# Projection weights laid out in memory one unit at a time, 4 KB in a row per partition

## What is computed

```python
mod = c @ w_ada + b_ada
shift, scale, gate = jnp.split(mod, 3, axis=-1)
h = rmsnorm(x, pre_norm_gain) * (1.0 + scale[:, None, :]) + shift[:, None, :]
proj = h @ w_in                                   # w_in: 1024 x 10840
(aq, ak, av, az, iq, ik, iw, bq, bk, bv, bz, bbeta, ba, ga, gb) = jnp.split(proj, points, axis=-1)
...
y_a = (o_a * jax.nn.silu(az)) @ w_a_out           # sparse attention, top 128 keys by an indexer
y_b = o_b.reshape(b, s, B_V_WIDTH) @ w_b_out      # gated delta rule in chunks
y = jax.nn.sigmoid(ga) * y_a + jax.nn.sigmoid(gb) * y_b
out = y @ w_o
return x + gate[:, None, :] * rmsnorm(out, post_norm_gain)
```

## Time and profile before

| | us |
|---|---|
| median of 3 runs | 827.98 (827.45 to 828.1) |
| profiled execution, span from first to last instruction | 824.1 |
| PE busy | 797.4 |
| PE weight load (beside the matmuls) busy | 639.8 |
| DVE, ACT, POOL busy | 439.9, 330.6, 393.3 |
| DMA queue's share of 16 engines' span | 40.2% |

### The profile page before, as it was taken

How to read it: one execution, slowest core, us unless ns; L and a number is a source line. 1 busy time by engine, 2 the same in 40 slices (tenths; PEclk the granted TensorE clock), 3 DMA queues, 4 the chain that set the end, 5 groups by cost and what they waited for, 6 DMA issues and landing times.

```text
span 824.1 us, 11189 instructions
## 1 busy us (share of the span) xinstructions
PE 797.4 (97%) x4060; PEld 639.8 (78%) x4060; DVE 439.9 (53%) x957; ACT 330.6 (40%) x701; POOL 393.3 (48%) x338
## 2 busy tenths in 40 slices
PE   6899899999999999999999999999999999999997
PEld 2377775787887888888887777777778788878997
DVE  5677779848779855776754333343343332331113
ACT  0557455543544435445335334424443322122231
POOL 0415643465545644545554453554365355434451
PEclk9999999999999999999999999999999999999999
DMA  8936656543344333333212212222222255542602
GB/s 314 345 104 213 163 116 168 157 118 104 95 82 113 72 103 104 89 89 90 78 51 78 78 52 76 83 74 75 77 77 73 61 173 182 176 128 77 215 17 102
DMA packets 166800, 95.61 MB, mean 116 GB/s; under 512 B 35009, under 2 KB 158274, under 8 KB 165722
## 3 DMA queue, kind: packets, MB, share of 16 engines
q1 hardware_dynamic: 166746, 94.91, 40.2%
HBM read 85.11 MB, written 9.22 MB: 114 GB/s over the span
## 4 chain that ended last, share of the span: by engine, by line
PE 77%; DVE 11%; DMA 4%; ACT 4%; issue 2%; SPq 1%; POOL 1%; DVEq 0%; POOLq 0%; ACTq 0%
PE ps L699 19%; PE ps L701 18%; PE ps L700 18%; DMA w_ada_sb<-in_w_ada 2%; PE ps L979 2%; PE ps L1030 2%; PE ps L1029 2%; PE ps L1028 2%; PE ps L966 2%; ACT prob L1278 2%; DVE prob L1917 1%; PE ps L973 1%; PE ps L817 1%; DVE kraw L1734 1%; PE ps L863 1%
## 5 line engine op out<-in xcount | busy, mean ns | idle before, releaser
L1376 POOL TENSOR_TENSOR w_lo<-raw,w_hi 128x512 fp32r<-128x512 f32 (+1 forms) x216 | 294.7, 1388 | 305.0 <-ACT w_hi L1052 289.6
L699 PE MATMUL ps<-h_hi,w_hi 128*128 128x512 f32 (+1 forms) x680 | 286.2, 421 | 1.1 <-DVE h_lo L1597 1.0
L701 PE MATMUL ps<-h_hi,w_lo 128*128 128x512 f32 (+1 forms) x680 | 266.7, 392 | 0.0
L700 PE MATMUL ps<-h_lo,w_hi 128*128 128x512 f32 (+1 forms) x680 | 265.4, 390 | 0.0
L699 PEld LDWEIGHTS ps<-h_hi,w_hi 128*128 128x128 f32 (+1 forms) x680 | 127.8, 188 | 32.1 <-issue 8.3
L701 PEld LDWEIGHTS ps<-h_hi,w_lo 128*128 128x128 f32 (+1 forms) x680 | 127.3, 187 | 28.8
L700 PEld LDWEIGHTS ps<-h_lo,w_hi 128*128 128x128 f32 (+1 forms) x680 | 128.1, 188 | 23.0 <-issue 2.2
L1052 ACT ACTIVATE w_hi<-raw 128x1024 fp32r<-128x1024 f32 (+1 forms) x109 | 113.6, 1051 | 19.4 <-PE ps L1030 17.1
L1218 ACT ACTIVATE o_tok<-ps 128x128 f32<-128x128 f32 x32 | 8.9, 278 | 92.8 <-PE ps L931 92.7
L1029 PE MATMUL ps<-w_lo,y_hi 128*128 128x256 f32 x128 | 36.2, 283 | 0.0
L1030 PE MATMUL ps<-w_hi,y_lo 128*128 128x256 f32 x128 | 36.2, 283 | 0.0
(11 more groups left out here) (276 smaller groups left out, 1330.7 us busy)
## 6 DMA issues: line engine op xcount, KB each, us to landing
raw<-in_w_in SPq DMA_DIRECT2D x84, 512.0 KB, 3.7
w_ada_sb<-in_w_ada SPq DMA_DIRECT2D x8, 1024.0 KB, 11.4
inverse_tiles<-zero SPq DMA_DIRECT2D x12, 344.0 KB, 4.8
raw<-in_w_b_out SPq DMA_DIRECT2D x8, 512.0 KB, 3.8
raw<-in_w_a_out SPq DMA_DIRECT2D x8, 512.0 KB, 3.8
ada<-in_w_ada SPq DMA_DIRECT2D x8, 512.0 KB, 5.0
raw<-in_w_o SPq DMA_DIRECT2D x8, 512.0 KB, 3.8
x_sb<-in_x SPq DMA_DIRECT2D x4, 512.0 KB, 20.0
```

The lines of the kernel that those rows point to most:

```text
L699: pe.matmul(out_ap, w_hi[:, slot, k, 0:m], rhs_hi(k), start=(k == 0), stop=False)
L700: pe.matmul(out_ap, w_hi[:, slot, k, 0:m], rhs_lo(k), start=False, stop=False)
L701: mm = pe.matmul(out_ap, w_lo[:, slot, k, 0:m], rhs_hi(k), start=False, stop=(k == KT - 1))
L1376: ins = pool.tensor_tensor(w_lo[:, slot, ks, 0:n], raw[:, slot, ks, 0:n], w_hi[:, slot, ks, 0:n].bitcast(F32), ALU.subtract)
```

## The change

The host hands over one new array, `w_units`, in place of the four matrices: unit by unit, each as `[128 partitions, 8, 128]`, so that a partition's 4 KB lie in a row and a unit is one block of 512 KB. Unit S is padded with zeros from 88 to 128 columns and read by the same `load`, in one DMA instead of two, so that its semaphore counts as the others' do. ACT, POOL and PE still use 88 columns of it. Nothing else is moved.

```diff
@@ -497,29 +497,11 @@
         sp.dma_start(small_cols[:, 48:56], a_log.rearrange("(a n) -> a n", a=1).to_broadcast([P, 8])).then_inc(s_sc, 16)
         sp.dma_start(small_cols[:, 56:64], dt_bias.rearrange("(a n) -> a n", a=1).to_broadcast([P, 8])).then_inc(s_sc, 16)
 
-        def columns(w, col):
-
-            return w.rearrange("(k p) n -> p k n", p=P)[:, :, col:col + P]
-
-        wv = w_in.rearrange("(k p) n -> p k n", p=P)
-        n_ik = IDX_DIM + IDX_HEADS
-        sp.dma_start(raw[:, 0, :, 0:n_ik], wv[:, :, COL_IK:COL_IK + n_ik]).then_inc(s_raw[0], 16)
-        sp.dma_start(raw[:, 0, :, n_ik:N_SMALL], wv[:, :, COL_BETA:COL_BETA + 2 * HEADS]).then_inc(s_raw[0], 16)
-        FIRST = {"K": COL_BK, "Q": COL_BQ, "V": COL_BV, "Z": COL_BZ, "I": COL_IQ, "GA": COL_GA, "GB": COL_GB, "AQ": COL_AQ,
-                 "AK": COL_AK, "AV": COL_AV, "AZ": COL_AZ}
-
         def load(q):
 
-            kind, n = UNITS[q]
-            if kind in FIRST:
-                src = columns(w_in, FIRST[kind] + n * P)
-            elif kind == "O":
-                src = columns(w_o, OUT_COLS[n])
-            else:
-                src = columns(w_b_out if kind == "BO" else w_a_out, n * P)
             if q >= RING:
                 sp.wait_ge(lo_made, q - RING + 1)
-            sp.dma_start(raw[:, q % RING, :, :], src).then_inc(s_raw[q % RING], 16)
+            sp.dma_start(raw[:, q % RING, :, :], w_units[q]).then_inc(s_raw[q % RING], 16)
 
         def clear(ns):
             sp.wait_ge(*pro_pool.at("zero"))
@@ -627,6 +609,7 @@
             sp.dma_start(ada[0][:], b_ada[2 * D:3 * D].rearrange("(a n) -> a n", a=1).to_broadcast([P, D])).then_inc(s_bc, 16)
             sp.dma_start(ada[1][:], post_gain.rearrange("(a n) -> a n", a=1).to_broadcast([P, D])).then_inc(s_bc, 16)
 
+        load(0)
         load(1)
         sp.dma_start(cst[:, 1:, :], cst_in[:, 1:, :]).then_inc(s_cst, 16)
         for q in range(2, RING):
@@ -1040,7 +1023,7 @@
         def split(q, n=P):
 
             slot = q % RING
-            act.wait_ge(s_raw[slot], (q // RING + 1) * 16 + (16 if slot == 0 else 0))
+            act.wait_ge(s_raw[slot], (q // RING + 1) * 16)
             if q == 0:
                 act.wait_ge(*pro_act.at("cos"))
                 act.wait_ge(*pro_act.at("sinI"))
@@ -2025,8 +2008,26 @@
                     *norm_dve.inc(f"x{n}{t}"))
 
 
-NAMES = ["x", "c", "positions", "w_ada", "b_ada", "pre_norm_gain", "post_norm_gain", "w_in", "idx_k_ln_gain",
-         "idx_k_ln_bias", "dn_conv_w", "dn_a_log", "dn_dt_bias", "dn_norm_gain", "w_a_out", "w_b_out", "w_o"]
+NAMES = ["x", "c", "positions", "w_ada", "b_ada", "pre_norm_gain", "post_norm_gain", "idx_k_ln_gain",
+         "idx_k_ln_bias", "dn_conv_w", "dn_a_log", "dn_dt_bias", "dn_norm_gain"]
+FIRST_COL = {"K": COL_BK, "Q": COL_BQ, "V": COL_BV, "Z": COL_BZ, "I": COL_IQ, "GA": COL_GA, "GB": COL_GB, "AQ": COL_AQ,
+             "AK": COL_AK, "AV": COL_AV, "AZ": COL_AZ}
+
+
+def unit_weights(q, w_in, w_a_out, w_b_out, w_o):
+
+    kind, n = UNITS[q]
+    if kind == "S":
+        w = np.zeros((D, P), np.float32)
+        w[:, 0:SM_BETA] = w_in[:, COL_IK:COL_IK + SM_BETA]
+        w[:, SM_BETA:N_SMALL] = w_in[:, COL_BETA:COL_BETA + 2 * HEADS]
+    elif kind in FIRST_COL:
+        w = w_in[:, FIRST_COL[kind] + n * P:FIRST_COL[kind] + (n + 1) * P]
+    elif kind == "O":
+        w = w_o[:, OUT_COLS[n]:OUT_COLS[n] + P]
+    else:
+        w = (w_b_out if kind == "BO" else w_a_out)[:, n * P:(n + 1) * P]
+    return w.reshape(KT, P, P).transpose(1, 0, 2)
 
 
 def kernel(**inputs):
@@ -2045,6 +2046,8 @@
         a = np.asarray(inputs[name])
 
         add(name, a if name in ("c", "positions") else a[0])
+    weights = [np.asarray(inputs[name])[0] for name in ("w_in", "w_a_out", "w_b_out", "w_o")]
+    add("w_units", np.stack([unit_weights(q, *weights) for q in range(len(UNITS))]))
     for name, a in zip(("masks", "rotary"), constants()):
         add(name, a)
     args.append(nc.dram_tensor("out", (S, D), F32, kind="ExternalOutput").ap())```

The new array is made before the launch, on the host. How SP's list changes, at the start of the program. Before (the numbers behind L are lines of the kernel before, `raw` is the ring of loaded weights, `cst` constants, `gc_rows` the decay rows in memory, `L` their copies on chip):

```order
L498 DMA small_cols<-in_dn_dt_bias 128x8
L506 DMA raw<-in_w_in 128x8x72
L507 DMA raw<-in_w_in 128x8x16
L522 DMA raw<-in_w_in 128x8x128
L631 DMA cst<-in_masks 128x896
L522 DMA raw<-in_w_in 128x8x128 x6
L528 DMA inverse_tiles<-zero 128x688 x3
L522 DMA raw<-in_w_in 128x8x128 x2
L639 DMA gc_rows<-gcT 8x512
L531 DMA L<-gc_rows 128x512 x4
```

More of the change, by code:

```diff
@@ L144, in inc, with build, program @@
         return self.sem, 1
-def build(nc, x, c, positions, w_ada, b_ada, pre_gain, post_gain, w_in, ln_gain, ln_bias, conv_w, a_log, dt_bias,
-          norm_gain, w_a_out, w_b_out, w_o, cst_in, cols_in, out):
+def build(nc, x, c, positions, w_ada, b_ada, pre_gain, post_gain, ln_gain, ln_bias, conv_w, a_log, dt_bias,
+          norm_gain, w_units, cst_in, cols_in, out):
     with ExitStack() as ctx:
[L150 to L155, removed]
+        program(nc, ctx, x, c, positions, w_ada, b_ada, pre_gain, post_gain, ln_gain, ln_bias, conv_w, a_log,
+                dt_bias, norm_gain, w_units, cst_in, cols_in, out)
+def program(nc, ctx, x, c, positions, w_ada, b_ada, pre_gain, post_gain, ln_gain, ln_bias, conv_w, a_log,
+            dt_bias, norm_gain, w_units, cst_in, cols_in, out):
     cursor = [-(-nc.sbuf_base // 64) * 64]
```

## The result

The changed kernel takes 829.82 us in the median of 20 runs (827.37 to 833.29), the kernel before, run beside it, 827.58 (826.87 to 832.28). The ratio is 1.0029, its 95% interval 1.0017 to 1.0040: 2.2 us slower, where I had forecast 827.2 us (825.8 to 829.0) and no visible change. (The ratios in this text are those on record for the runs; the quotient of the two medians differs from them by up to 0.1%.) The profiled execution spans 830.5 us (824.1 before); like those of before it is one execution of many, and a rather long one, so its 6.4 us are read as places where time is lost, and their worth in the median comes from the runs.

What follows compares the result with a forecast made beforehand. TensorE bounds the kernel, busy 797.4 of 824.1 us; prologue -0.6 and decay rows -0.2 give 823.3 in the profile, so the runs' median 827.98 - 0.8 = 827.2 us, range 825.8 to 829.0, no visible change.

Steps and rivals of the forecast that it cites:

- Step 3: Decay rows: the gc_rows store behind a unit load lands 0.4 us sooner, DVE can use 0.24: -0.2 us.
- Steps 1 and 4: SyncE's load issues, and all unit loads after the prologue, hidden beneath PE work: 0 us each.
- the signs of being wrong: ACT waiting for later units, first h_hi after 39.9, w_ada's landing moved, PE idle from 100 to 300 us changed over 1 us.
- step 2: Prologue: S and K0 land earlier, POOL's w_lo end sooner, the first h_lo ends at 41.1 instead of 41.7: -0.6 us.
- The 0.35 us for the two broadcasts: Prologue: time assumed for two 4 KB broadcasts queued ahead of S, chosen between 0 and 1 us.
- -0.85 to +0.2: Prologue bounds: POOL gone before h_lo is due, -0.85 us; both x_sb operations and h_lo held by POOL, +0.2 us.
- It gives back what it gains: Rival: POOL and DVE trade hold-ups in the prologue, or only S changes; 0 to -0.3 us, 827.7 to 828.2; chance 0.25.
- The slower rival: Prologue: slow loads land K0 after 38.4, its ACT conversion delays the first h_hi; 830.6 us at 130 GB/s; chance 0.10.

Runs made afterwards that it cites:

- e3: Changed kernel with the first four units (S, K0, 2, 3) loaded as before the change, the other 105 from the new array; 827.90 us, ratio 1.0006.
- e7: Changed kernel with three of the seven constant blocks loaded ahead of S and K0, S converted at 34.53; 828.33 us, ratio 1.0012.
- e5: Changed kernel with seven instead of three unused matmuls on PE behind the conditioning, while it waits for x_sb; 829.21 us, ratio 1.0017.
- e4: Only the first four units (S, K0, 2, 3) read from the new array, the other 105 from the old matrices; 830.44 us, ratio 1.0038.
- e8: Kernel of e2 with four instead of three unused matmuls on PE behind the conditioning; 828.25 us, ratio 1.0005.
- e1b: The same kernel as e1, run once more; 827.33 us, ratio 0.9997.
- e3b: The same kernel as e3, run once more; 827.65 us, ratio 0.9993.
- e2: Changed kernel with POOL waiting for the fourth x_sb before it makes w_lo of S and K0; 826.95 us, ratio 0.9998.
- e2b: The same kernel as e2, run once more; 827.21 us, ratio 1.0004.
- e1: Changed kernel with the load of the constants (448 KB) issued ahead of S and K0 instead of behind them; 828.47 us, ratio 1.0022.
- e6: Only unit S read from the new array, padded, in one load; all others, K0 too, from the old matrices; 828.97 us, ratio 1.0016.

## Why the prediction was wrong

**Right, by its own terms.** Rate (407 taken, 406 to 410 read), packets, the landing of `w_ada`, and no wait of ACT for a unit after the prologue. S and K0 were forecast at 34.3 and 35.6 and converted at 34.07 and 35.36. Step 3 came as sized: DVE's L starts 2.15 us late behind a start that was 2.36 late, -0.2 us, without its wait of 0.24, and L813's gap is 2.1 us (2.3 forecast). The issue of a 4 KB-row load, for which I had kept 0.1 us, is not longer but shorter: 0.33 us in the median against 0.37. Steps 1 and 4 stand at 0 by e3: 105 of 109 units in the new layout change nothing that can be told. Of the signs of being wrong that I had named, two came: the first h_hi at 42.33 (later than 39.9), and PE's idle time from 100 to 300 us up by 1.4 us, 5.9 against 4.5, with one of the half clocks and the wait for vnew in it; PE's busy time grew by 3.9 us, where 1 was allowed.

**The step that failed is step 2**, the replay of POOL and DVE, forecast at -0.6 us with +0.2 as its worst. Measured at the end of the first h_lo it is +2.0 us. I had the mechanism, turns of whole instructions, and missed three things.

- *Who takes part.* I replayed x_sb and h_lo only. L1577 and L1579 (L1560 and L1562 now) stood directly ahead, at 35.41 and 35.62 with 0.17 and 0.16 us, too short to look dangerous; but each reads two operands from on-chip memory, and each can wait for a whole 0.8 to 1.26 us operation of POOL. They lost 0.28 + 0.69 us, and pushed the third x_sb from 35.81 to 36.90, into K0's two longer operations. So both x_sb waited, where before one did: 3.38 - 2.09 = 1.29 us more. The sum, with 0.1 us for a later `mod`, is the 2.4 us of the first profile.
- *When it starts.* The 0.35 us for the two broadcasts was a choice; ACT's S stood 0.28 us earlier than by it. In e7, 0.46 us later than in the changed kernel, one of the two short operations escaped. With the right start but without the two operations my replay would have said at most the +0.2 of its bound, which was for S at 33.7.
- *What follows.* "-0.85 to +0.2" had no term for PE. In its wait of 4.1 us instead of 1.8 its clock fell, in the chain (0.5 us by e5) and in later stretches in some executions. The prediction read 1.00 throughout in one execution and counted on it.

The Trainium skill's page "SBUF — State Buffer", section "Who interferes with whom", says in general what the first bullet found: GpSimd and VectorE share a pair of ports, whoever issues first has it for the whole instruction, the other blocks, and a VectorE instruction with two inputs in that memory contends with a GpSimd instruction that reads there. The rows of the two short ones agree, 0.17 to 0.45 us and 0.16 to 0.85 us; e7 agrees too, where the one that came ahead of POOL kept its 0.17. The x_sb scaling reads one tensor only; the page has `tensor_scalar` contend in a 2-port mode, and that it ran in one is shown by no run here, only that it waited (1.72 and 1.75 us).

**The rivals.** "It gives back what it gains" named the place, but not that it could give back more. The slower rival had the right sign and a wrong mechanism: ACT's queue and slow rows (under 194 GB/s), where the rows were fast and ACT waited for DVE. The mechanism that decided stood in my text as a bound of +0.2.

**What stays open.** How the median's 2.2 us divide between the wait and the clock. Besides a half clock in its last 5 us, which every profile has, all six profiles with a late x_sb (the changed kernel twice, e4 to e7) have at least one; of the eight with x_sb in time only e8 has one. Mean clocks are on record for most executions: the 30 of the changed kernel average a clock of 0.9946, with 15 at 0.994 or less; 97 of the kernel before average 0.9972, with 7. At equal clock, 0.996 to 0.998, the changed kernel's executions are 0.8 to 1.5 us slower on average (9 against 63), at 0.995 not at all (6 against 4), and e5, at before's mean clock, is 1.8 us slower on average. So I estimate roughly 1 to 1.8 us for the wait, and the rest for the clock that falls more often behind it; why it falls in one execution and not in another is open.

The runs that kept before's times in the prologue (e1b, e3, e3b) or held POOL back (e2, e2b) are within 0.1% of before, e1 alone came out at 1.0022, unexplained; with e4's 1.0038 for the first four units by themselves I put the median's loss as a whole down to the prologue.

## What to carry to other kernels

A faster transfer off the critical path is not free of effect: ask what it lets start, on which engine, and next to what; here the weights' second split, wanted only by 42 us, began 1 us sooner and cost the path 2.4 in the first profile. In such a replay list every instruction of the neighbour engine in the stretch, the shortest too, since a turn costs the length of the other's operation and not one's own. Where the late starter has slack, a wait that holds it back (one line in e2) takes away the loss of the faster load; a gain it did not bring here.

## What the runs showed that I had not expected

- Operations of 0.17 and 0.16 us became 0.45 and 0.85 us beside POOL's, up to five times as long, and the same numbers to the hundredth in three kernels (the changed one, e4 and e5).
- Half the delay of landing (e7) took away a third of DVE's loss only: the loss goes in steps, by operations met.
- PE's granted clock fell to 0.50 for 3.41 us (6.83 in e4 and e6) around a wait of 2.9 to 4.1 us: 3.4 us into it in the changed kernel, 2.3 and 2.0 us into it in e4 and e6, 0.8 us behind it in the repetition of the changed kernel, and not at all in e7 with a wait of 3.4; in the later places it fell behind waits of 1.9 and 2.1 us, while the kernel before kept 1.00 after its 2.5 us gap in its profile.
- More idle products for PE (e5) kept the clock up at 40 us but gave only 0.5 us.
